# The first norm of an encoder kernel in two halves of columns, with copies and sums in another order and a gate row on GpSimd

## What is computed

```python
cond = jax.nn.silu(c)
mod = cond @ ada_w[l] + ada_b[l]
sh_a, sc_a, g_a, sh_f, sc_f, g_f = jnp.split(mod, 6, axis=-1)
h = modulate(rms_norm(x, norm_attn[l]), sh_a, sc_a)   # h * (1 + scale) + shift
y = diff_attention(h, a_w_qkv[l], ..., a_w_o[l], rel_bias, lam_init)
x = x + g_a[:, None, :] * y
h = modulate(rms_norm(x, norm_ffn[l]), sh_f, sc_f)
y = swiglu(h, ffn_w_in[l // 2], ffn_w_out[l // 2])    # layer 0
```

## Time and profile before

| | |
|---|---|
| median of 3 runs | 1528.77 us (1524.25 to 1528.91) |
| the profiled execution: its own time | 1525.94 us |
| its span | 1524.1 us |
| PE busy | 1466.6 us, 96% |
| DVE busy | 1292.8 us, 85% |
| ACT busy | 979.9 us, 64% |
| POOL busy | 130.7 us, 9% |
| moved by DMA | 494.37 MB, 324 GB/s |

### The profile page before, as it was taken

One profiled execution on the slowest core, in us unless ns is written; L12 is line 12 of the kernel. 1 busy time (PEld: TensorE's weight loads), 2 busy tenths in 40 slices (PEclk: granted clock), 3 DMA queues, 4 the chain that ended last, 5 costly groups with the idle time before them and its releaser, 6 DMA issues.

```text
span 1524.1 us, 22197 instructions
## 1 busy us (share of the span) xinstructions
PE 1466.6 (96%) x6546; PEld 1152.2 (76%) x6546; DVE 1292.8 (85%) x1383; ACT 979.9 (64%) x1249; POOL 130.7 (9%) x143
## 2 busy tenths in 40 slices
PE   6998889999999999999999999999999999999997
PEld 2774667777677678888888888888888888888885
DVE  6888779988776788898898898888889889888896
ACT  3557343444556466777777777677777777777773
POOL 3000122211119000000000000000000000000100
PEclk9999999999999999999999999999999999999999
DMA  9984489998743479999999999999999999999993
GB/s 355 371 294 148 153 296 388 384 369 299 193 152 111 152 252 361 373 374 381 366 364 382 367 360 390 364 356 391 370 361 381 371 363 372 366 360 372 396 394 121
DMA packets 212228, 494.37 MB, mean 324 GB/s; under 512 B 16433, under 2 KB 39185, under 8 KB 212177
## 3 DMA queue, kind: packets, MB, share of 16 engines
q1 hardware_dynamic: 196848, 440.46, 79.6%
q0 software_dynamic: 14528, 51.22, 9.5%
q10 hardware_dynamic: 802, 2.06, 0.4%
HBM read 487.13 MB, written 6.55 MB: 324 GB/s over the span
## 4 chain that ended last, share of the span: by engine, by line
PE 90%; DVE 5%; ACT 2%; DMA 2%; issue 1%; SPq 0%; DVEq 0%; ACTq 0%
PE PS L1694 87%; PE PS L2211 2%; DMA WRAW<-in_ada_w 1%; DVE MOD L1094 1%; DVE WLO L1080 1%; PE PS L1744 1%; PE PS L1817 0%; DVE HT_LO L1153 0%; PE PS L2189 0%; DMA WRAW<-in_a_w_o 0%; DVE X L1236 0%; DVE H L1235 0%; SPq L439 0%; PE PS L1994 0%; DVE ss L1160 0%
## 5 line engine op out<-in xcount | busy, mean ns | idle before, releaser
L1080 DVE TENSOR_TENSOR WLO<-WRAW,WHI 128x1024 fp32r<-128x1024 f32 x790 | 915.7, 1219 | 39.1 <-ACT WHI L697 38.5
L697 ACT ACTIVATE WHI<-WRAW 128x1024 fp32r<-128x1024 f32 x790 | 779.6, 1052 | 90.9 <-PE PS L1694 70.0
L1694 PE MATMUL PS<-WHI,HT_HI 128*128 128x512 f32 x1280 | 516.0, 403 | 9.9 <-DVE HT_LO L1153 6.4
L1694 PE MATMUL PS<-WLO,HT_HI 128*128 128x512 f32 x1280 | 508.0, 397 | 0.0
L1694 PE MATMUL PS<-WHI,HT_LO 128*128 128x512 f32 x1280 | 434.4, 396 | 0.0
L1694 PEld LDWEIGHTS PS<-WHI,HT_HI 128*128 128x128 f32 x1280 | 241.6, 189 | 67.6 <-DVE WLO L1080 7.2
L1694 PEld LDWEIGHTS PS<-WHI,HT_LO 128*128 128x128 f32 x1280 | 241.1, 188 | 58.8
L1694 PEld LDWEIGHTS PS<-WLO,HT_HI 128*128 128x128 f32 x1280 | 241.7, 189 | 55.1 <-issue 0.5
L1694 PE MATMUL PS<-WHI,AT_HI 128*128 128x512 f32 x536 | 216.7, 404 | 3.0 <-DVE AT_LO L1375 1.6
L1694 PE MATMUL PS<-WLO,AT_HI 128*128 128x512 f32 x536 | 211.7, 395 | 0.0
L1694 PE MATMUL PS<-WHI,AT_LO 128*128 128x512 f32 x536 | 211.7, 395 | 0.0
(11 more groups left out here) (222 smaller groups left out, 860.5 us busy)
## 6 DMA issues: line engine op xcount, KB each, us to landing
WRAW<-in_moe_w_in SPq DMA_DIRECT2D x448, 512.0 KB, 6.4
WRAW<-in_moe_w_out SPq DMA_DIRECT2D x224, 512.0 KB, 5.5
WRAW<-in_ada_w SPq DMA_DIRECT2D x48, 512.0 KB, 8.8
SHR<-in_ada_w POOLq DMA_DIRECT2D x48, 512.0 KB, 6.6
WRAW<-in_ffn_w_in SPq DMA_DIRECT2D x88, 256.0 KB, 7.9
WRAW<-in_a_w_qkv SPq DMA_DIRECT2D x24, 512.0 KB, 12.9
WRAW<-in_ffn_w_out SPq DMA_DIRECT2D x22, 512.0 KB, 6.3
SHR<-in_kv_ada_w POOLq DMA_DIRECT2D x16, 512.0 KB, 6.8
```

Of the source, the lines that this page charges most:

```text
L697: nc.scalar.activation(WHI[:, u.split(k), :], WRAW[:, u.raw(k), :], ACT.Copy).then_inc(w_hi, 1)
L1080: V_.tensor_tensor(WLO[:, u.split(k), :], WRAW[:, u.raw(k), :], f32(WHI[:, u.split(k), :]), ALU.subtract).then_inc(w_lo, 1)
L1694: return nc.tensor.matmul(out, a, b, start=start, stop=stop)
```

## The change

Rows 1 and 0 are each loaded and used in two halves of 512 columns. A piece now holds 512 columns of two weight rows per partition, 2 KB runs; four make a half. The ring begins with the scale's first half, the shift's first half and units 0 to 3; then come the scale's second half, unit 4, the shift's second half, unit 5. DVE multiplies the scale pieces (`scale_products`, 512 columns each); all shift pieces are multiplied on PE (`first_shift`, eight matmuls for a half). The first half of H is finished and transposed (units 0 to 3 need no more), PE projects units 0 to 2, sums the second half of the scale, projects unit 3, multiplies the second half of the shift, does six fill matmuls, transposes the second half and goes on with unit 4.

The gate's eight products move from DVE to POOL: four ahead of the load of the bias table, four behind it. POOL's wait for 14 splits goes; its load of the biases now waits for 16 scale products. On ACT, the exponential of lambda moves behind the first copies, K's transposes are copied ahead of units 24 and 25, and units 26 and 27 are copied behind the first exponentials. On DVE the splits 24 to 27 and one product change places with the first two `biased`. The sum of row 3 moves from behind step (0,5) to behind step (1,2), and the split of unit 36 behind a difference of the activations.

The diff, cut ("..." marks what is left out: new semaphores, context, and signatures that follow from the rest):

```diff
...
-EARLY_PE = ((0, 3), (0, 7))
+SCALE_A = [[("scale_a", half, pair) for pair in range(KT // 2)] for half in range(2)]
+SHIFT_A = [[("shift_a", half, pair) for pair in range(KT // 2)] for half in range(2)]
+EARLY_PE = SHIFT_A[0] + SHIFT_A[1]
+EARLY_DVE = SCALE_A[0] + SCALE_A[1]
+A_UNITS = 4
...
-    order = [(1, k) for k in range(KT)] + [(0, k) for k in range(KT)]
+    order = SCALE_A[0] + SHIFT_A[0]
     for n in range(3 * KT):
+        if n == A_UNITS:
+            order += SCALE_A[1]
+        if n == A_UNITS + 1:
+            order += SHIFT_A[1]
...
-POOL_PIECES = [("gate_f", k) for k in range(KT)]
...
+POOL_PIECES = [(2, k) for k in range(KT)] + [("gate_f", k) for k in range(KT)]
+DVE_PIECES = [what for what in RING if isinstance(what, tuple) and what not in PE_PIECES + POOL_PIECES + EARLY_DVE]
...
                     sp.wait_ge(ada_pe, PE_PIECES.index(what) + 1)
+                elif what in EARLY_DVE:
+                    sp.wait_ge(scale_used, 2 * EARLY_DVE.index(what) + 2)
...
-            for c in (1, 0):
-                for k in range(KT):
-                    load_piece((c, k), t["ada_w"][0], c * D)
+            def load_half(pieces, col):
+                for what in pieces:
+                    place, half, k = PLACE[what], what[1], 2 * what[2]
+                    slot_read(place - RAW_SLOTS)
+                    c = col + half * 512
+                    sp.dma_start(WRAW[:, place % RAW_SLOTS, :].rearrange("p (k n) -> p k n", k=2),
+                                 t["ada_w"][0].rearrange("(p k) n -> p k n", p=P)[:, k:k + 2, c:c + 512]
+                                 ).then_inc(w_landed[place % RAW_SLOTS], 16)
...
+            load_half(SCALE_A[0], D)
+            load_half(SHIFT_A[0], 0)
...
+                    if n == A_UNITS:
+                        load_half(SCALE_A[1], D)
+                    if n == A_UNITS + 1:
+                        load_half(SHIFT_A[1], 0)
...
-            pool.wait_ge(ada_used, 10)
+            pool.wait_ge(scale_used, 2 * KT)
...
-            pool.wait_ge(w_lo, 14)
...
-            load_bias()
-            pool.wait_ge(bias_landed, 16 * TOEP_HEADS)
-            pool.memset(BIAS[0:64, :, 192:256], NEG).then_inc(bias_masked, 1)
...
+            pool.wait_ge(modb_landed, 32)
+            pool_products(MOD[:, MOD0[2], :], 0, 4)
+            load_bias()
+            pool_products(MOD[:, MOD0[2], :], 4, KT)
+            pool.wait_ge(bias_landed, 16 * TOEP_HEADS)
+            pool.memset(BIAS[0:64, :, 192:256], NEG).then_inc(bias_masked, 1)
...
-            pool_products(MOD[:, MOD1[5], :])
+            pool_products(MOD[:, MOD1[5], :], KT, 2 * KT)
...
+                    hi(Units(U_QKV), 26, 27)
...
-            act.wait_ge(sq_read, 1)
-            nc.scalar.activation(neglam[:, 0:2], neglam[:, 0:2], ACT.Exp).then_inc(sq_ready, 1)
...
-            hi(u, 0, 1)
-            ht_his(0, BY_HALF)
+            hi(u, 0)
+            ht_his(0, BY_HALF[:2])
+            hi(u, 1, 2)
+            act.wait_ge(sq_read, 1)
+            nc.scalar.activation(neglam[:, 0:2], neglam[:, 0:2], ACT.Exp).then_inc(sq_ready, 1)
+            load_table(ACT.Sqrt)
+            hi(u, 3, 4)
+            ht_his(0, BY_HALF[2:])
...
-            hi(u, *range(2, 14))
+            hi(u, *range(5, 14))
...
+            transposed(4, lambda n: K[:, n // 2, (n % 2) * 512:(n % 2) * 512 + 512], 1, range(0, 4), qkt_psum)
+            load_table(ACT.Exp)
             hi(u, 24, 25)
-            transposed(4, lambda n: K[:, n // 2, (n % 2) * 512:(n % 2) * 512 + 512], 1, range(0, 4), qkt_psum)
-            hi(u, 26, 27)
-            load_table(ACT.Exp)
...
-                if c < 2 and k == 0:
-                    V_.tensor_scalar(row, piece, condT[:, k:k + 1], None, ALU.mult).then_inc(ada_used, 1)
-                else:
-                    V_.scalar_tensor_tensor(row, piece, condT[:, k:k + 1], row, ALU.mult, ALU.add
-                                            ).then_inc(ada_used, 1)
+                V_.scalar_tensor_tensor(row, piece, condT[:, k:k + 1], row, ALU.mult, ALU.add
+                                        ).then_inc(ada_used, 1)
...
+            def scale_products(half, pairs):
+                row = MOD[:, MOD0[1], half * 512:half * 512 + 512]
+                for pair_of_k in pairs:
+                    place = PLACE[SCALE_A[half][pair_of_k]]
+                    dve.wait_ge(w_landed[place % RAW_SLOTS], landed_at(place))
+                    for c in range(2):
+                        k = 2 * pair_of_k + c
+                        piece = WRAW[:, place % RAW_SLOTS, c * 512:c * 512 + 512]
+                        if k:
+                            dve.wait_ge(scale_used, half * KT + k)
+                            V_.scalar_tensor_tensor(row, piece, condT[:, k:k + 1], row, ALU.mult, ALU.add
+                                                    ).then_inc(scale_used, 1)
+                        else:
+                            V_.tensor_scalar(row, piece, condT[:, k:k + 1], None, ALU.mult).then_inc(scale_used, 1)
...
+            def first_scaled(half, bank):
+                cols = slice(half * 512, half * 512 + 512)
+                dve.wait_ge(mod_sum, half + 1)
+                dve.wait_ge(gain_first, 16)
+                V_.scalar_tensor_tensor(MOD[:, MOD0[1], cols], PS[:, bank, :], 1.0, GB[:, cols],
+                                        ALU.add, ALU.mult).then_inc((fold_half, gain_used)[half], 1)
+                dve.wait_ge((fold_half, gain_used)[half], 1)
+                for i in range(TB):
+                    chain(V_.scalar_tensor_tensor(H[:, i, cols], X[:, i, cols], nx[:, i, 1:2],
+                                                  MOD[:, MOD0[1], cols], ALU.mult, ALU.mult))
...
+            def first_shifted(half, bank):
+                cols = slice(half * 512, half * 512 + 512)
+                dve.wait_ge(ada_pe, len(SHIFT_A[0]) * (half + 1))
+                for i in range(TB):
+                    V_.tensor_tensor(H[:, i, cols], H[:, i, cols], PS[:, bank, :], ALU.add).then_inc(h_ready, 1)
...
-            for n in range(0, 4):
-                early_product(n)
+            scale_products(0, range(KT // 2))
+            await_root()
+            chain(V_.reciprocal(nx[:, :, 1:2], nx[:, :, 1:2]))
+            dve.wait_ge(toep_mm, NBIAS // TOEP_HEADS)
+            first_scaled(0, 6)
             dve.wait_ge(lam_landed, 16)
             lv = lamv.rearrange("p (a b d) -> p a b d", a=2, b=2)
             chain(V_.tensor_tensor(lv[:, :, 0, :], lv[:, :, 0, :], lv[:, :, 1, :], ALU.mult))
             V_.tensor_reduce(neglam[:, 0:2], lv[:, :, 0, :], axis=AX, op=ALU.add).then_inc(sq_read, 1)
-            for n in range(4, KT):
-                early_product(n)
-            for n in range(KT, KT + 2):
-                early_product(n)
-            await_root()
-            chain(V_.reciprocal(nx[:, :, 1:2], nx[:, :, 1:2]))
-            dve.wait_ge(mod_sum, 2)
-            fold(MOD0[1], pair(6), 1)
-            dve.wait_ge(cst_landed, 16)
+            first_shifted(0, 4)
+            u = Units(U_QKV)
+            lo(u, 0)
+            ht_los(0, BY_HALF[:2])
+            lo(u, 1)
+            scale_products(1, range(0, 1))
+            lo(u, 2)
+            scale_products(1, range(1, 3))
+            lo(u, 3)
+            scale_products(1, range(3, 4))
+            lo(u, 4)
+            first_scaled(1, 0)
+            first_shifted(1, 2)
+            ht_los(0, BY_HALF[2:])
+            lo(u, 5)
             chain(V_.tensor_tensor(MOD[:, 5, 0:P], ident, iota, ALU.mult))
             chain(V_.tensor_reduce(tokf[:, :], MOD[:, 5, 0:P], axis=AX, op=ALU.add))
             V_.tensor_copy(tokid[:, 0, :], tokf[:, :].broadcast_to([P, 2]))
             V_.tensor_scalar(tokid[:, 1, :], tokf[:, :].broadcast_to([P, 2]), float(P), None, ALU.add).then_inc(ey_ready, 1)
-            for n in range(KT + 2, 2 * KT - len(EARLY_PE)):
-                early_product(n)
-            dve.wait_ge(toep_mm, NBIAS // TOEP_HEADS)
-            dve.wait_ge(gain_used, 1)
-            for i in range(TB):
-                chain(V_.scalar_tensor_tensor(H[:, i, :], X[:, i, :], nx[:, i, 1:2], MOD[:, MOD0[1], :],
-                                              ALU.mult, ALU.mult))
-            dve.wait_ge(ada_pe, len(EARLY_PE))
-            for half in range(2):
-                cols = slice(half * 512, half * 512 + 512)
-                for i in range(TB):
-                    V_.tensor_tensor(H[:, i, cols], H[:, i, cols], PS[:, 4 + half, :], ALU.add
-                                     ).then_inc(h_ready, 1)
-            u = Units(U_QKV)
-            lo(u, 0)
-            ht_los(0, BY_HALF)
-            lo(u, 1)
             dve.wait_ge(modb_landed, 32)
-            rest = iter(range(2 * KT - len(EARLY_PE), DVE_EARLY))
+            rest = iter(range(DVE_EARLY))
...
-            lo(u, 2, 3)
-            for k in range(4, 14):
-                lo_and_products(k, k in GATE_AT)
+            for k in range(A_UNITS + 2, 14):
```

(70 more changed lines are left out.)

## The result

| | before | after |
|---|---|---|
| median | 1528.3 us (16 runs, 1522.66 to 1530.51) | 1531.62 us (16 runs, 1523.9 to 1535.18) |
| ratio | | 1.0024, 95% interval 1.0014 to 1.0035 |
| profiled execution | 1525.94 us | 1526.27 us |
| its span | 1524.1 us | 1524.4 us |

What follows compares the result with a forecast made beforehand. PE was taken as the bound, busy 1010.8 of 1024 us from 500 us on. Terms +1.7 - 1.9 + 0.6 - 4.7 = -4.3 us took 1525.94 to 1521.6; with the median 2.8 above, 1524.5, range 1518.5 to 1531.

Steps and rivals of the forecast that it cites:

- Rival D: Gate row's stage: DVE and GpSimd block each other, making splits wait; +9 us, 1538; chance 0.08.
- rival C: GpSimd's chain ends late: mask after 108, unit 22 landing after 101; four us late gives 1528; chance 0.12.
- step 3: Gate row on GpSimd: mask by 104, needed at about 108; cost 0, or +1 for each us beyond 108.
- Step 1: First norm by halves: first projection at 29.0 us instead of 40.43, range 27.3 to 31.3, a gain of 11.4.
- Step 2: Between projection units 3 and 4: 13.1 us of PE work inserted, Q and K projections end +1.7 later (0 to +4).
- Step 4: V stage, K's copies first: fifth head's bias 1.9 us earlier (bounds -5.0 to +1), plus 0.6 for half clock.
- term of the cold clock: V stage: PE idles 3 us before the first transpose, then some 4 us at half clock; +0.6 us.
- Step 5: w_o stage: shift sum moved so PE no longer waits for DVE's products; -4.7 us (bounds -5.5 to -2).

Runs made afterwards that it cites:

- gate_dve: Changed kernel with the gate row's eight products put back on VectorE at their old places; 0.9970 of before.
- halves_only: Kernel before with only the first norm by halves added; 1.0035 of before.
- gate_only: Kernel before with only the gate row's eight products moved to GpSimd, four ahead of the bias loads and four behind; 0.9977 of before.
- early_pool: Changed kernel with GpSimd's wait before its bias and gain loads shortened from all sixteen scale products to the first half's eight; 0.9979 of before.
- pool_write: Changed kernel with each gate product on GpSimd replaced by six memsets that read nothing (gate row zero); 1.0030 of before.
- pool_tt: Changed kernel with each gate product on GpSimd cut to its two-input sum alone, without the scaling; 1.0005 of before.
- copies_only: Kernel before with only ScalarE's copies of Q and K moved ahead and VectorE's splits of units 24 and 25 behind the first head's bias; 0.9992 of before.
- orders_only: Kernel before with the three changes of order (copies, shift sum, splits of units 36 and 37), no halves, gate row not on GpSimd; 0.9959 of before.
- sum_only: Kernel before with only the feed-forward's shift sum moved from behind the attention's fifth pair to behind the second; 0.9949 of before.

## Why the prediction was wrong

It said 1524.5 us with 1518.5 to 1531.0 and 0.10 for slower; 1531.62 is above the range. Rival D's sign came true, by rival C's mechanism. The step that failed is step 3, the cost of 0 for the gate row on GpSimd. The top of the range, too, is less than its own terms give: rival C's 1528 and 4.7 make 1532.7.

**Step 1, first projection at 29.0.** Measured 31.30, and 29.4 to 32.9 over the kernels with halves. The failed term is "the scale products end by about 14.2 ..., so these six wait for nothing". The bias row did come early, as the choice of 29.0 assumed (PE starts at 12.29 instead of 15.00), but that gain was lost again: the fourth piece of 2 KB rows was read at 16.27, where 12.88 was counted on. PE idled 1.81, and then the two sum matmuls and the shift products took 2.08 and 7.92, against 1.13 and 7.03 in gate_dve, whose idle time was 1.07. The granted clock is 1.00 in both traces, so why they took longer is not shown.

**Step 2, 13.1 inserted.** Right: K end is 58.09 after the first projection, 45.15 before, so 12.94 were inserted. With step 1's miss the sum is +3.8 instead of +1.7, and halves_only shows that the whole part loses (1.0035, 5.3 us). The argument "The early start is more than paid back here" was right and not drawn to its end: the halves should have been costed as a clear loss.

**Step 3, gate row at cost 0.** This is the step that failed. Each of its terms was short: the bias DMA went out at 41.84 (39 said), the chain began at 59.44 (57 said), a product took 6.6 us on average (5.4 said), the mask came at 115.9 (104 said) and unit 22 was issued at 96.0 (87 said). The later start and eight times 1.2 make the 12 us by which the mask is late, against 4 of slack. C's condition (mask after 108, unit 22 after 101) held, but C was priced for a chain 4 us late only. What the runs show in place of 0 is a loss of some 8 us against gate_dve (1.0024 against 0.9970). The step's own price, "+1 for each us beyond 108", gives 7.9 for a mask at 115.9, so it was the schedule that was wrong more than the price; that the two agree so well is in part luck, for the price was set on the mask and the last to come was a V unit. Early and in the old kernel the row on GpSimd gains 3.5 us (gate_only), early and beside the halves nothing that can be measured (0.9979 in early_pool, 0.9970 in gate_dve).

**Rival D** gave the lock too small a chance for a wrong reason. The earlier trace rows show a split starting 1.18 us into a one-input instruction of GpSimd and running for its usual time. In the changed kernel it is the two-input sum that holds a split to its end (3.22 and 3.32 us). The one-input instruction is itself drawn out, to 4.75, and holds a split or a product for less: 2.05 to 2.13 us where it holds one at all. The rule cited there, from the Trainium skill ("SBUF — State Buffer", section "Who interferes with whom"), agrees with this trace for the sum: the later one is blocked, 3.22 us for a split of 1.22. For the one-input instruction it agrees in part only. The section also says that a GpSimd instruction that only writes does not contend; the 1219 ns of pool_write agree. But the lock acted on the time mostly through GpSimd's own pace. Of D's waits that PE feels, the changed kernel has the two of 1.79 and 1.26 in the V stage, with a longer wait behind them; they decided only in pool_tt.

**Step 4, V stage -1.9, and +0.6 for the clock.** Not decided. In copies_only the fifth head's bias stood 35.0 after K end (34.2 said, 36.1 before): 1.1 gained where 1.9 was said. But w_o came 1.6 later, with 0.54 of the clock granted from 120 to 130 us behind PE's wait of 3.00; by that execution the term of the cold clock is 2.7, not 0.6. In orders_only, with the same copies, 0.87 was granted there and w_o came 0.5 earlier. The ratio of copies_only, 0.9992, is a gain of 1.2 us, between a gain of 3.7 and a loss of 1.2, and the -1.3 forecast lies within. Beside the gate row the copies bring nothing: leaving them alone took the ratio from 0.9938 to 0.9913.

**Step 5, -4.7.** Right for the stage: 4.9 in sum_only. The time fell by 7.8, which is open. Missed beside it: the split of unit 36 behind the activations' difference, "0", took 2.7 off the wait before the feed-forward and gave 1.7 back.

Put together by ratios, halves +0.35%, orders -0.41% and gate row -0.23% make -0.29%; the change gave +0.24%. The halves and the orders together, gate_dve, gave -0.30% (adding gives -0.06%, a difference at the edge of the noise), so what does not add is above all the gate row: -0.23% by itself, +0.54% on top of gate_dve. The halves moved the event that GpSimd's queue waits for from 25.43 to 41.84. Shortening that wait returned 0.45%; the 0.09% left is within the noise.

## What to carry to other kernels

When work is put at the end of another engine's queue, first write down when that queue gets going: here one wait for sixteen products instead of ten, harmless for the small loads it was made for, delayed a chain of eight products by over 10 us, and through the ring everything behind it. Where slots are given back in strict order, cost an added reader by its latest read, and its pace with something on top where the row of its duration is from a stage with other company. And try the parts of a change one by one: two of the four here were gains of 0.2 and 0.5%, one was not told from nil, one a loss of 0.35%, and the sum hid all of them. Then try them together, for a gain by itself (the gate row) was none beside the halves.

## What was not expected of the hardware

- A two-input sum on GpSimd lasts 2.4 us alone and holds a two-input instruction of VectorE to its end: in the changed kernel splits of 1.22 that started in its first 0.4 us took 3.2 to 3.4, a product of 1.28 took 3.42. A one-input instruction on GpSimd is itself drawn out, from 2.85 to 3.70 or 4.75 us, and what ran beside it on VectorE there took either its usual time or 2.05 to 2.13. Sums without a pause between them took 3.2 to 3.3 us each (pool_tt), and the splits beside them 3.42 or 3.43. Memsets do neither (1.219).
- The same two matmuls of a sum took 1.12 or 1.13 us behind 1.07, 1.68 and 1.69 us of idle time, and 2.08 behind 1.81, 2.02, 2.03 and 2.42 (four executions). The granted clock's column showed 1.00 there even so; in pool_tt, where they took 1.45, it showed 0.60 from 18.5 to 20 us. The length of the idle time does not decide alone: in the kernel before, four records of such a sum took 1.98 behind 1.82, the pace of the quick ones.
